# Decode value pages issued from ScalarE's DMA queue instead of SyncE's

## The reference

```python
gate = jnp.einsum('bhqd,bnhd->bhqn', q.astype(jnp.float32), kmean)
_, sel = lax.top_k(gate, n_sel)
phys = blk_pages[jnp.arange(Bd)[:, None, None, None], sel]
...
k_sel = cache_k[phys, hidx].reshape(Bd, H, L, n_sel * MOBA_BLOCK, D)
v_sel = cache_v[phys, hidx].reshape(Bd, H, L, n_sel * MOBA_BLOCK, D)
...
p = jax.nn.softmax(jnp.concatenate(s_parts, axis=-1), axis=-1)
...
    term = (jnp.einsum('bhqk,bhqkd->bhqd', pp, vals) if per_query
            else jnp.einsum('bhqk,bhkd->bhqd', pp, vals))
```

## Time and profile before

| What | Value |
|---|---|
| Time, median of 3 runs | 2635.54 us (2633.23 to 2636.22) |
| The profiled execution's own time | 2636.08 us |
| Its span | 2634.3 us |
| Granted TensorE clock, mean | 0.984 |
| TensorE busy | 2515.5 us (95%) |
| VectorE busy | 1126.8 us (43%) |
| ScalarE busy | 684.6 us (26%) |
| DMA, mean rate | 132 GB/s, 347.76 MB |

### The profile page before, as it was taken

How to read it: one execution, slowest core, us unless ns; L and a number is a source line. 1 busy time by engine, 2 the same in 40 slices (tenths; PEclk the granted TensorE clock), 3 DMA queues, 4 the chain that set the end, 5 groups by cost and what they waited for, 6 DMA issues and landing times.

```text
span 2634.3 us, 52234 instructions
## 1 busy us (share of the span) xinstructions
PE 2515.5 (95%) x20592; PEld 2396.9 (91%) x20592; DVE 1126.8 (43%) x1842; ACT 684.6 (26%) x1197; POOL 120.8 (5%) x265
## 2 busy tenths in 40 slices
PE   8999999888789988999999999999999999999994
PEld 8999999854469988999999999999999999999994
DVE  6523234422143349444444343444444444434357
ACT  5212222400022224322222222222222222222231
POOL 3000000000000005000000000000000000000002
PEclk9999999999999989999999999999999999999997
DMA  5487775378854221322322232222223222222231
GB/s 171 157 293 255 259 250 191 111 277 326 321 204 163 86 65 61 91 88 81 92 88 88 84 92 87 86 85 88 87 80 96 88 88 80 95 85 87 84 98 76
DMA packets 146652, 347.76 MB, mean 132 GB/s; under 512 B 16608, under 2 KB 16608, under 8 KB 146048
## 3 DMA queue, kind: packets, MB, share of 16 engines
q1 hardware_dynamic: 144480, 338.35, 38.5%
q0 software_dynamic: 2080, 8.14, 0.8%
HBM read 334.32 MB, written 12.10 MB: 132 GB/s over the span
## 4 chain that ended last, share of the span: by engine, by line
PE 86%; SPq 5%; DVE 4%; DMA 2%; issue 1%; DVEq 1%; ACT 1%; POOL 0%
PE ps_acc L777 30%; PE ps_acc L754 16%; PE ps_a L777 15%; PE ps_b L777 15%; PE ps_a L826 4%; SPq L365 3%; SPq L369 1%; DMA region<-vcache 1%; PE ps_a L754 1%; PE ps_b L754 1%; PE ps_b L870 1%; DVE w_lo L313 1%; DVE act_lo L1057 1%; PE ps_b L900 1%; DMA w_raw<-units 0%
## 5 line engine op out<-in xcount | busy, mean ns | idle before, releaser
L313 DVE TENSOR_TENSOR w_lo<-w_raw,w_hi 128x512 fp32r<-128x512 f32 x724 | 501.5, 704 | 1074.9 <-ACT w_hi L307 1071.5
L307 ACT ACTIVATE w_hi<-w_raw 128x512 fp32r<-128x512 f32 x724 | 445.5, 628 | 1280.9 <-PE ps_acc L777 474.6
L777 PE MATMUL ps_acc<-act_hi,w_hi 128*128 128x272 f32 x1472 | 309.0, 292 | 24.3 <-DVE act_lo L1057 17.4
L777 PE MATMUL ps_acc<-act_lo,w_hi 128*128 128x272 f32 x1472 | 307.7, 290 | 0.0
L777 PE MATMUL ps_acc<-act_hi,w_lo 128*128 128x272 f32 x1472 | 305.6, 289 | 0.0
L754 PE MATMUL ps_acc<-act_hi,w_hi 128*128 128x272 f32 x1280 | 274.3, 296 | 2.1 <-DVE region L1231 1.4
L754 PE MATMUL ps_acc<-act_hi,w_lo 128*128 128x272 f32 x1280 | 265.2, 289 | 0.0
L754 PE MATMUL ps_acc<-act_lo,w_hi 128*128 128x272 f32 x1280 | 264.8, 288 | 0.0
L777 PEld LDWEIGHTS ps_acc<-act_hi,w_hi 128*128 128x128 f32 x1472 | 233.2, 190 | 27.0 <-issue 12.6
L777 PEld LDWEIGHTS ps_acc<-act_hi,w_lo 128*128 128x128 f32 x1472 | 234.2, 190 | 0.0
L777 PEld LDWEIGHTS ps_acc<-act_lo,w_hi 128*128 128x128 f32 x1472 | 234.0, 191 | 0.0
(11 more groups left out here) (221 smaller groups left out, 3723.2 us busy)
## 6 DMA issues: line engine op xcount, KB each, us to landing
w_raw<-units SPq DMA_DIRECT2D x724, 256.0 KB, 2.6
region<-kcache SPq DMA_DIRECT2D x128, 512.0 KB, 4.4
region<-vcache SPq DMA_DIRECT2D x128, 512.0 KB, 6.7
region<-xT SPq DMA_DIRECT2D x8, 544.0 KB, 6.5
region<-xT SPq DMA_DIRECT2D x4, 1088.0 KB, 8.5
yT<-region SPq DMA_DIRECT2D x8, 544.0 KB, 2.7
ext_out<-region POOLq DMA_DIRECT2D x8, 339.5 KB, 6.1
kT_out<-scratch POOLq DMA_DIRECT2D x8, 272.0 KB, 5.1
```

The costliest lines, as they stand in the source:

```text
L307: act.activation(w_hi[:, s], w_raw[:, s], ACT.Copy).then_inc(hi_ready, 1)
L313: dve.tensor_tensor(w_lo[:, s], w_raw[:, s], w_hi[:, s].bitcast(F32), ALU.subtract).then_inc(lo_ready, 1)
L777: mm = pe.matmul(banks(mt, odd)[:, n, 0:HN], w[:, s, i, cols], half(a[:, kt], n), start=kt == 0 and w is w_hi and a is hi, stop=kt == 2 * ...
```

## The change

`load_values` and the two places in the loop that call it leave SP's stream and enter ScalarE's, unchanged but for the engine. SP keeps the weight units and the key pages. In ScalarE's loop the calls stand right behind the split of the step, ahead of all other work of the step. The registers are now ScalarE's, as are the register loads, the waits on page_used and the 128 page issues.

```diff
--- before.py
+++ after.py
@@ sync @@
-            by_half = table.rearrange("(b a) p -> b a p", a=2)
-
-            def load_values(R, h):
-
-                i, r = divmod(R, PAGES)
-                if r % 2 == 0 and h == 0:
-                    sp.load(pg, by_half[4 * i:4 * i + 4, r // 8, r % 8:r % 8 + 2])
-                sp.wait_ge(page_used, 61 + 2 * R + h)
-                for q in (2 * h, 2 * h + 1):
-                    page = sp.snap(pg[2 * q + r % 2], min_val=0, max_val=N_PHYS - 1)
-                    sp.dma_start(pages[:, 4 * (R % 2) + q], vcache[bass.ds(page, 1)].rearrange("a p n -> p (a n)"))\
-                        .then_inc(page_loaded[2 * (R % 2) + h], 16)
-
@@ sync, the loop over p @@
                 load_unit(sp, 8, p + RING)
                 for m in pairs_at(p + 1):
                     load_pair(m)
-                if 60 <= p < 64:
-                    load_values((p - 60) // 2, p % 2)
-                for R in rounds_at(p + 1):
-                    if R >= 2:
-                        for h in range(2):
-                            load_values(R, h)
@@ scalar @@
+            pg = [act.alloc_register(f"value{i}") for i in range(8)]
+            by_half = table.rearrange("(b a) p -> b a p", a=2)
+
+            def load_values(R, h):
+
+                i, r = divmod(R, PAGES)
+                if r % 2 == 0 and h == 0:
+                    act.load(pg, by_half[4 * i:4 * i + 4, r // 8, r % 8:r % 8 + 2])
+                act.wait_ge(page_used, 61 + 2 * R + h)
+                for q in (2 * h, 2 * h + 1):
+                    page = act.snap(pg[2 * q + r % 2], min_val=0, max_val=N_PHYS - 1)
+                    act.dma_start(pages[:, 4 * (R % 2) + q], vcache[bass.ds(page, 1)].rearrange("a p n -> p (a n)"))\
+                        .then_inc(page_loaded[2 * (R % 2) + h], 16)
+
             load_q(0)
             for p in range(WEAVE):
                 s, u = divmod(p, 8)
                 split_hi(act, 8, p + LEAD)
+                if 60 <= p < 64:
+                    load_values((p - 60) // 2, p % 2)
+                for R in rounds_at(p + 1):
+                    if R >= 2:
+                        for h in range(2):
+                            load_values(R, h)
```

## The result

The changed kernel takes 2638.85 us (median of 20 runs, 2636.87 to 2643.22); the kernel before took 2634.92 on the same chip (20 runs, 2631.00 to 2637.39). The ratio is 1.0019, with a 95% interval of 1.0012 to 1.0025: slower by some 4 to 5 us, where 4 us less were predicted. That is inside the predicted range, and the size is under 0.2%, but the sign is the other one. The profiled execution took 2640.23 us, with a span of 2638.4. Of all runs told here one, a run of the kernel before with its page numbers in one row, took 2760.67 us at a granted clock of 0.842, where the others had 0.98, and is left out of its median.

What follows compares the result with a forecast made beforehand. The first queue's own instructions, mainly register loads, were taken to set the pace from 541 to 745 us. Terms -8.3 + 1.4 + 1.1 + 0.5 + 0.5 + 1 = -3.8 took 2636.08 to 2632.3 us; range 2612 to 2655.

Steps and rivals of the forecast that it cites:

- the unit issues: Weight-unit issues staying on SP, so leaving the chain of page issues: 17 x 0.49 = 8.3 us saved.
- the splits: Weight splits on ScalarE ahead of page issues: 17 x 0.08 = +1.4 us, up to +11.9 at the other end.
- the page issue on ScalarE: About 108 chained page issues, now on ScalarE: taken as +0 us, between 0 and +22.
- the dear page issue: Rival: ScalarE's page issue costs POOL's 0.539 us, +22 us, 2654 us; chance 0.20 together with a dearer register load.
- the held sequencer: Rival: register load or issue waits for ScalarE's split, or the queues meet every step; some 2640 to 2642 us; chance 0.15.
- The signs asked for: Profile signs: ScalarE's queue in the chain, SP waiting for w_lo, R = 3 to second values_end shortening from 214.6 to 210 us.
- two queues that get in each other's way: Unit issues on SP beside page issues on ScalarE: +1 us taken, 4 or 9 if they collide more.
- the sentence on the register load: Register loads of page numbers on ScalarE: price kept at 8.4 us, so +0; far ends -56 and +34 us.
- step 75: Third register load, done by SP at 526 to 531, comes on ScalarE only after the split at 536.13: +0.5 us.
- values_end(0): On ScalarE once in mid-stretch; the next split cannot start before it ends: +1.1 us.
- Dearer register load: Rival: register loads cost more on ScalarE, +8 us and more; chance 0.20 together with the dear issue.
- The transfers close their gaps: Rival: pages on their own queue run faster until transfer rate limits the stretch; half 2618, all 2601 us; chance 0.18.

## Why the prediction was wrong

**What was right.** The bound: the first queue's own instructions set the pace, the register load first among them, and after the change the same instructions do so on ScalarE. The size of the unit issues (-9.6 for -8.3), of the splits (+2.1 for +1.4, the load of the next step starting within the split), and of the page issue on ScalarE (340 ns for 333, +1.1 for 0) came out as worked. So two rivals fell: the dear page issue and the held sequencer. SP waits for w_lo (194.1 us in 19 waits), and the trace shows no wait of TensorE for w_lo from 541 us on. The signs asked for came in part: R = 3 goes out 0.83 us later, as foreseen, but from there to the second values_end it is 219.8 us and not some 210.

For two queues that get in each other's way I had taken +1 us, between 0 and 9. The Trainium skill (Perfetto Trace Analysis, section "DMA Instruction — HWDGE (DVE, Sync)") says that the block that makes descriptors is locked by one issue at a time. The trace shows no price of it: 7 of the 19 unit issues ran while a page issue ran, and all 19 took 327 or 328 ns. The unit issue's median fell from 439 to 328 ns, and the page issue's rose by 7 ns.

**The step that failed** is the sentence on the register load: "It reads the same addresses under the same traffic, so I take 8.4". That term was 0 and measured +12.1 us. The traffic is not the same, because the load's start against its own pages is part of it. The queue time that the change took out between the pages and the next load lets the load start with more of them still queued, 3.00 MB where 2.75 were. Moving the units alone shows this on SP, with 2.98 MB queued: 6.4 of 9.6 us came back in the loads. So about half of the +12.1 is shown without ScalarE having a part; the other half is not. The sum treated the 117 us of loads as a constant, so that all of the unit issues' time could be saved; in the runs, queue time ahead of a load is partly free already. The prediction had the hint, a rate of 391 GB/s that falls to 121 at the end of a load, and used it for a rival that would gain from closing these gaps, not to ask what sets the load's length.

**The second mis-sized term** is step 75, taken as +0.5. Its times were foreseen to 0.6 us (pages of round 2 near 541.3 and found at 541.9, the next load unmoved and found 0.5 later). (One reading was off and carries no term: of the 15.3 us of page_used waits in the earlier trace rows, 6.7 ended at 538; 8.6 lie in the stretch.) What was not foreseen is that the next load, with round 2's and round 3's pages out together in front of it, takes 9.9 us and not 7.5. Moving that one load two steps earlier brought the kernel from 1.0019 to 1.0004. A smaller term was too high: values_end(0), taken as +1.1, held the queue for some 0.1 us: it started at 646.41, ran 1.1 us, and the next page was issued at 646.65.

With the -2.8 us of the units moved alone as what the relief of the queue is really worth, some +3 to +4 from step 75 and about +3 from splits and page issues (2.1 + 1.1), one arrives at +3 to +4.5, near the +3.9 between the medians. That is a sum of separate runs, each uncertain by 2 to 3 us, and the page issues' 1.1 may be counted in step 75 as well; it is no proof of the parts. Open is why the loads on ScalarE stay at 9.17 us on average with step 75 mended, against 8.84 on SP with only the units moved and as many pages queued, and whether a unit asked for beside the load adds to them.

**The rivals.** "Dearer register load" stood in one clause with the dear issue, at +8 and more; the sign was right, the size was not, and that the engine makes the load dearer, which was the reason, is not shown. "The transfers close their gaps" did not happen by this change, and did by the one that took the loads away: -33 us, close to the whole of that rival's 35.

## What to carry to other kernels

The price of a load from DRAM into registers hangs on the traffic around it (here 4.4 us in light traffic, 8.4 to 9.3 under pages): price it by the traffic queued when it starts, and expect it to lengthen when the queue in front of it is relieved. When the chain is held by such a load, remove the load (here, one transfer of all page numbers to SBUF at the start: 33 us) before choosing the queue that issues it. When a sequence moves to an engine with work of its own, look for the step that the old queue could do early and the new one cannot; one late load made most of the difference here.

## What the runs showed of the hardware

- A load of eight numbers cost by pieces and by traffic: 0.53 us from SBUF; 0.87 us from one row of DRAM in light traffic (the shortest on SP, at 452 us), and a median of 1.9 to 2.4 under pages; in four pieces 3.1 to 3.5 in light traffic and 5.2 to 5.7 under pages (medians of the two kernels compared). The read of the pointer before it took 1.24 us in light traffic; in the runs with full pages and four pieces its median was 3.1 to 4.1. The Trainium skill (Runtime: NRT & Kernel Launch, section "Instruction fetch mechanics") gives about 200 ns for each register. For eight that is an estimate of 1.6 us by that page. The rows here lie on both sides of it, for the place, the pieces and the traffic decide.
- ScalarE's sequencer starts a register load 0.01 to 0.02 us after its split starts, while the split runs for 0.63 us (as at 546.08 in the changed kernel).
- Without the loads from DRAM, pages and units on two queues were as good as on one: 2602.62 and 2601.86 us.
